# Recurrence gates in mixed PSUM banks: seven gate tiles per group of three channel chunks instead of ten

## The reference, cut to what matters

```
xb, gate = split(rmsnorm(x) @ w_in)                  # 1024 -> 2 x 1536
xb = causal_depthwise_conv(xb)                       # 4 taps
xs = xb.reshape(seq, 16 blocks, 96)
r = sigmoid(einsum('shi,hij->shj', xs, wr) + br)     # 16 blocks of 96 x 96
i = sigmoid(einsum('shi,hij->shj', xs, wi) + bi)
log_a = -8 * r * softplus(-lam);  a = exp(log_a)
b = sqrt(1 - a^2) * (i * xb)
hs[t] = a[t] * hs[t-1] + b[t]
x = x + (hs * silu(gate)) @ w_out
```

## Time and profile before

| what | us |
|---|---|
| median of 3 runs | 1112.67 |
| lowest and highest | 1112.06, 1564.1 |
| the profiled execution, its own time | 1113.04 |
| its span in the trace | 1111.2 |
| PE busy | 1098.6 (99%) |
| DVE busy | 769.9 (69%) |
| ACT busy | 558.6 (50%) |
| POOL busy | 249.9 (22%) |

### The profile page before, as it was taken

One profiled execution on the slowest core, in us unless ns is written; L12 is line 12 of the kernel. 1 busy time (PEld: TensorE's weight loads), 2 busy tenths in 40 slices (PEclk: granted clock), 3 DMA queues, 4 the chain that ended last, 5 costly groups with the idle time before them and its releaser, 6 DMA issues.

```text
span 1111.2 us, 14419 instructions
## 1 busy us (share of the span) xinstructions
PE 1098.6 (99%) x5216; PEld 867.9 (78%) x5216; DVE 769.9 (69%) x1220; ACT 558.6 (50%) x953; POOL 249.9 (22%) x226
## 2 busy tenths in 40 slices
PE   8999999999999999999999999999999999999997
PEld 6787787887677778867777878888878888888886
DVE  7887978787667765465445545547797687787796
ACT  6666567565676644254434433325453443453455
POOL 2022111330323412032112210003330440440443
PEclk9999999999999999999999999999999999999999
DMA  6322323323111123311222222223501701702401
GB/s 224 121 76 76 100 91 108 102 94 105 58 58 58 58 77 114 105 58 57 95 76 96 76 76 95 95 96 114 208 20 38 265 20 46 257 1 74 173 1 76
DMA packets 30054, 103.79 MB, mean 93 GB/s; under 512 B 3488, under 2 KB 3872, under 8 KB 29984
## 3 DMA queue, kind: packets, MB, share of 16 engines
q1 hardware_dynamic: 29552, 102.26, 26.8%
q10 hardware_dynamic: 432, 0.62, 0.2%
HBM read 100.24 MB, written 2.10 MB: 92 GB/s over the span
## 4 chain that ended last, share of the span: by engine, by line
PE 89%; DVE 6%; ACT 2%; issue 2%; DMA 1%; POOL 0%; SPq 0%; DVEq 0%; POOLq 0%; ACTq 0%
PE ps L903 22%; PE ps L904 22%; PE ps L905 22%; PE ps L863 4%; PE ps L864 4%; PE ps L865 4%; PE ps L1007 3%; PE ps L1022 3%; PE ps L1053 2%; DVE wl L1416 2%; PE ps L1047 1%; DMA raw<-wst 1%; DVE fl L1823 0%; PE ps L810 0%; DVE sg L1510 0%
## 5 line engine op out<-in xcount | busy, mean ns | idle before, releaser
L903 PE MATMUL ps<-xgh,wh 128*128 128x512 f32 x847 | 336.9, 398 | 1.8 <-ACT wh L1081 1.5
L905 PE MATMUL ps<-xgh,wl 128*128 128x512 f32 x847 | 330.3, 390 | 0.0
L904 PE MATMUL ps<-xgl,wh 128*128 128x512 f32 x847 | 330.0, 390 | 0.0
L1416 DVE TENSOR_TENSOR wl<-raw,wh 128x1024 fp32r<-128x1024 f32 x148 | 197.4, 1336 | 50.1 <-ACT wh L1092 49.5
L1092 ACT ACTIVATE wh<-raw 128x1024 fp32r<-128x1024 f32 x148 | 155.0, 1050 | 74.0 <-PE ps L905 53.8
L903 PEld LDWEIGHTS ps<-xgh,wh 128*128 128x128 f32 x847 | 159.1, 188 | 39.7 <-issue 6.5
L905 PEld LDWEIGHTS ps<-xgh,wl 128*128 128x128 f32 x847 | 159.0, 188 | 33.8
L904 PEld LDWEIGHTS ps<-xgl,wh 128*128 128x128 f32 x847 | 159.2, 188 | 32.4 <-issue 1.0
L1928 POOL TENSOR_SCALAR Pt<-Pt,stat 128x256 f32<-128x256 f32 (+2 forms) x128 | 75.0, 598 | 274.2 <-DVE stat L1672 199.0
L1300 ACT ACTIVATE Pt<-Pt,stat 128x256 f32<-128x256 f32 (+2 forms) x128 | 64.3, 503 | 60.9 <-DVE stat L1640 23.1
L863 PE MATMUL ps<-wh,fh 128*128 128x512 f32 x224 | 87.5, 391 | 1.9 <-DVE wl L1416 1.9
(11 more groups left out here) (244 smaller groups left out, 1798.6 us busy)
## 6 DMA issues: line engine op xcount, KB each, us to landing
raw<-wst SPq DMA_DIRECT2D x148, 512.0 KB, 3.5
b<-wdn SPq DMA_DIRECT2D x32, 512.0 KB, 6.8
bst<-nbias SPq DMA_DIRECT2D x8, 256.0 KB, 3.4
xt<-xT SPq DMA_DIRECT2D x3, 512.0 KB, 8.1
outT<-xtok SPq DMA_DIRECT2D x3, 512.0 KB, 2.6
sq<-fin SPq DMA_DIRECT2D x2, 256.0 KB, 4.3
cstt<-cst SPq DMA_DIRECT2D x1, 448.0 KB, 5.7
raw<-wst SPq DMA_DIRECT2D x1, 320.0 KB, 5.7
```

Source lines behind the costliest of these rows:

```text
L903: e.matmul(o, high, a, start=(k == 0), stop=False)
L904: e.matmul(o, high, b, start=False, stop=False)
L905: e.matmul(o, low, a, start=False, stop=stop).then_inc(tile_done, 1)
L1416: e.tensor_tensor(wl_t[:, v % NHL, :], src, f32(wh_t[:, v % NHL, :]), ALU.subtract).then_inc(lo_done, 1)
```

## The change: what it does, and the diff

A gate bank now holds halves of both gates. For each chunk one bank gets r of the chunk's lower 64 channels on partitions 0 to 63 and i of the same channels on partitions 64 to 127 (weights `r_i`), the other i of the upper 64 on partitions 0 to 63 and r of the upper 64 on 64 to 127 (`i_r`). The middle chunk needs then no full tile: its own 128 rows are two pieces of 64 rows with disjoint rows and different banks, one *pair* tile (pair 0), the pieces from its neighbours are pair 1, and what the neighbours need from it is pair 2. The low and the high chunk keep two full tiles each. In order: pair 0, full, full, pair 1, full, full, pair 2. The middle chunk is complete after the fourth tile, the low and the high one after the seventh.

ACT reads each chunk's two banks with four instructions on 64 partitions each (L1182 and L1185 before were one each on 128), two of which write to the other half of the partitions. The bias of i is stored rolled by 64 to lie beside its data.

The layer has 12 tiles fewer, one unit and a half. One unit keeps four tiles and is padded with zeros (`SHORT`), so that from the first tile of the next layer on the units hold the same tiles as before; in all there is one unit fewer. The ticks that depend on these places move: `gate_tick`, and the places of the unit splits in groups 1 to 3.

```
     def gates(self, g):
-        c = 3 * g
-        for own, over in (([("gr", c), ("gi", c)], 2), ([("gr", c + 1), ("gr", c + 2)], 0), ([], 3), ([("gi", c + 1), ("gi", c + 2)], 1)):
-            for name in own:
-                self.take(name)
-                self.tiles.append((name, 0, False))
...
+        middle, low, high = 3 * g, 3 * g + 1, 3 * g + 2
+        self.pair(g, 0, opens=(("gr", middle), ("gi", middle)))
+        self.full(low, "gr")
+        self.pair(g, 1, closes=(middle,))
+        self.full(high, "gi")
+        self.pair(g, 2, closes=(low, high))
+        for c in (middle, low, high):
+            self.n_act += 4
+            self.frees["gr", c] = ("act", self.n_act - 1)
+            self.frees["gi", c] = ("act", self.n_act)
...
         for g in range(4):
-            places = [end["silu", c] for c in range(3 * g, 3 * g + 3)] + [end["silu", 3 * g + 2] + 8]
+            ends = [end["silu", c] for c in range(3 * g, 3 * g + 3)] + [end["silu", 3 * g + 2] + 8]
+            taps = [ev_at["conv", c] + 2.0 for c in range(3 * g, 3 * g + 3)]
             if g == 0:
-                places = [end["conv", 2]] + places
+                places = [end["conv", 2]] + ends
+            elif g == 1:
+                places = [end["conv", 3]] + taps[1:] + ends
+            elif g == 2:
+                places = [end["conv", 6] - 3] + taps + ends
             else:
-                taps = [ev_at["conv", c] + 2.0 for c in range(3 * g, 3 * g + 3)]
-                places = [end["conv", 3 * g] - (3 if g > 1 else 0)] + taps + places[g < 2:]
+                places = taps + ends
...
-                UNIT_AT[u] = max(8.0 * u - 20.0, UNIT_AT[u - 1] + 5.0)
+                UNIT_AT[u] = max(ch.units[u][1] - 20.0, UNIT_AT[u - 1] + 5.0)
...
         def gate_tick(c):
-            return end["gi", c] + 1.2 + 3.5 * (c % 3 > 1)
+            return end["gi", c - c % 3] + 1.2 + (0.0, 3.0, 6.5)[c % 3]
...
-            def gates_over(g, n, high, low):
+            def gates_pair(g, n, high, low):
+                middle, below, above = 3 * g, 3 * g + 1, 3 * g + 2
+                if n == 0:
+                    bits = [(lo, middle, ("gr", middle)), (hi, middle, ("gi", middle))]
+                    for rows, k, name in bits:
+                        wait_bank(q, name)
+                elif n == 1:
+                    bits = [(slice(96, 128), below, ("gr", middle)), (slice(0, 32), above, ("gi", middle))]
+                    q.wait_ge(tile_done, ch.at_pair[g] + 1)
                 else:
+                    bits = [(lo, middle, ("gi", below)), (hi, middle, ("gr", above))]
...
             def gate(c):
-                e.activation(trr, bank[ch.bank["gr", c]], ACT.Tanh, scale=0.5, bias=drvc(HBR + c, HBR + c + 1)).then_inc(gate_read, 1)
-                q.wait_ge(tile_done, end["gi", c] + 1)
+                x_, y_ = bank[ch.bank["gr", c]], bank[ch.bank["gi", c]]
+                t_ = tii[c % 2]
+                r_, i_ = drvc(HBR + c, HBR + c + 1), drvc(HBI + c, HBI + c + 1)
+                e.activation(trr[lo, :], x_[lo, :], ACT.Tanh, scale=0.5, bias=r_[lo, :]).then_inc(gate_read, 1)
+                e.activation(trr[hi, :], y_[hi, :], ACT.Tanh, scale=0.5, bias=r_[hi, :]).then_inc(gate_read, 1)
                 q.wait_ge(ix_done, c - 1)
-                e.activation(tii[c % 2], bank[ch.bank["gi", c]], ACT.Tanh, scale=0.5,
-                             bias=drvc(HBI + c, HBI + c + 1)).then_inc(gate_read, 1)
+                e.activation(t_[lo, :], x_[hi, :], ACT.Tanh, scale=0.5, bias=i_[hi, :]).then_inc(gate_read, 1)
+                e.activation(t_[hi, :], y_[lo, :], ACT.Tanh, scale=0.5, bias=i_[lo, :]).then_inc(gate_read, 1)
```

More of the change, by code:

```diff
@@ L16 @@
 UT = 8
+SHORT = 4
 NRAW = 3
@@ L88, in __init__ @@
         self.end, self.ring, self.at, self.n_dve, self.n_act, self.user = {}, 7, 0, 0, 0, {}
-        self.at_over = {}
+        self.at_pair = {}
         self.units, self.unit_of = [], []
@@ L108, in run, with unit @@
             self.frees[name] = ("dve", self.n_dve)
[L110 to L114, removed]
+    def unit(self, kind, size, n=None):
+        stop = len(self.unit_of) + n if n else len(self.tiles)
+        while len(self.unit_of) < stop:
+            first = len(self.unit_of)
+            size = min(size, stop - first)
+            self.unit_of += [(len(self.units), s) for s in range(size)]
             self.units.append((kind, first, first + size - 1))
@@ L150, in gates, with full, pair @@
     def gates(self, g):
-        c = 3 * g
-        for own, over in (([("gr", c), ("gi", c)], 2), ([("gr", c + 1), ("gr", c + 2)], 0), ([], 3), ([("gi", c + 1), ("gi", c + 2)], 1)):
-            for name in own:
-                self.take(name)
-                self.tiles.append((name, 0, False))
[L158 to L166, removed]
+        middle, low, high = 3 * g, 3 * g + 1, 3 * g + 2
[8 more added lines that the diff above has]
+            self.frees["gi", c] = ("act", self.n_act)
+    def full(self, c, alone):
+        for kind in ("gr", "gi"):
+            self.take((kind, c))
+            self.tiles.append(((kind, c), 0, kind == alone))
+    def pair(self, g, n, opens=(), closes=()):
+        for name in opens:
+            self.take(name)
+        if n == 0:
+            self.at_pair[g] = len(self.tiles)
+        self.tiles.append((("pair", g, n), 0 if opens else 1, False))
+        for c in closes:
+            self.end["gr", c] = self.end["gi", c] = len(self.tiles) - 1
     def group(self, names, k, ks):
@@ L209, in gemm_plan @@
         ch.gates(g)
+    ch.unit(("ring",), UT)
     for j in range(6):
@@ L217, in gemm_plan @@
         ch.one(("wa", j), 12)
+    ch.unit(("ring",), SHORT, SHORT)
     ch.ring, ch.at = 3, 1
@@ L795, in conv_there @@
                 return xsh_t[:, c % 4, :], xsl_t[:, c % 4, :]
-            def gates_over(g, n, high, low):
[L799 to L802, removed]
-                else:
[L804 to L807, removed]
+            def gates_pair(g, n, high, low):
+                middle, below, above = 3 * g, 3 * g + 1, 3 * g + 2
+                if n == 0:
+                    bits = [(lo, middle, ("gr", middle)), (hi, middle, ("gi", middle))]
[4 more added lines that the diff above has]
+                    q.wait_ge(tile_done, ch.at_pair[g] + 1)
+                else:
+                    bits = [(lo, middle, ("gi", below)), (hi, middle, ("gr", above))]
                 bits = [(rows, *conv_there(k), bank[ch.bank[name]]) for rows, k, name in bits]
                 for rows, a, b, o in bits:
-                    e.matmul(o, high[rows], a[rows], start=False, stop=False)
+                    e.matmul(o, high[rows], a[rows], start=(n == 0), stop=False)
                 for rows, a, b, o in bits:
@@ L813, in gates_over @@
                 for rows, a, b, o in bits:
-                    done = e.matmul(o, low[rows], a[rows], start=False, stop=(n != 2))
+                    done = e.matmul(o, low[rows], a[rows], start=False, stop=(n != 0))
                 done.then_inc(tile_done, 1)
@@ L870, in gemm @@
                     u, s = ch.unit_of[t]
-                    if k == 0:
+                    if k == 0 and name[0] != "pair":
                         wait_bank(q, name)
@@ L889, in gemm @@
                     low = wl_t[:, u % NHL, blk(s)]
-                    if name[0] == "over":
-                        gates_over(name[1], name[2], high, low)
+                    if name[0] == "pair":
+                        gates_pair(name[1], name[2], high, low)
                         continue
@@ L1513, in gate @@
                 yield gate_tick(c) + 2.0
-                q.wait_ge(gate_read, 2 * c + 2)
+                q.wait_ge(gate_read, 4 * c + 4)
                 q.wait_ge(xsl_done, c + 1)
@@ L2037, in weight_stream, with r_i, i_r @@
         add(gate[3 * g:3 * g + 3])
[L2038 to L2051, removed]
+        def r_i(rows, first):
+            return np.concatenate([full[n, g, rows, first:first + 64] for n in (0, 1)], axis=1)
+        def i_r(rows, first):
+            return np.concatenate([full[n, g, rows, first:first + 64] for n in (1, 0)], axis=1)
+        pairs = np.zeros((3, 128, 128), np.float32)
+        pairs[0, 0:64], pairs[0, 64:128] = r_i(slice(128, 192), 128), i_r(slice(192, 256), 192)
+        pairs[1, 96:128], pairs[1, 0:32] = r_i(slice(96, 128), 128), i_r(slice(256, 288), 192)
+        pairs[2, 0:64], pairs[2, 64:128] = i_r(slice(128, 192), 64), r_i(slice(192, 256), 256)
+        add(pairs[0:1])
+        add(np.stack([r_i(slice(0, 128), 0), i_r(slice(0, 128), 64)]))
+        add(pairs[1:2])
+        add(np.stack([r_i(slice(256, 384), 256), i_r(slice(256, 384), 320)]))
+        add(pairs[2:3])
+    rest = wo[:2, 6:9].reshape(-1, 128, 128)
+    add(rest[:SHORT])
+    add(np.zeros((UT - SHORT, 128, 128), np.float32))
+    add(rest[SHORT:])
     add(wo[2:6, :9])
@@ L2111, in params @@
     put("br", cols(a["a_gate_r_b"][0])[:, CHUNKS])
-    put("bi", cols(a["a_gate_i_b"][0])[:, CHUNKS])
```

(1 more changed line is left out.)

4 lines of the change are left out of this document (2 added, 2 removed).

## The result

The changed kernel took 1130.27 us (median), the one before 1112.92 beside it: the ratio is 1.0157, with a 95% interval of 1.0145 to 1.017. It is slower by 17.3 us; forecast were 9.3 and at most 14. The profiled execution of the changed kernel took 1131.17 us, 0.9 more than the median; its span is 1129.2.

The account below looks back on a forecast made before the run. The loop of DVE, ACT and POOL was taken as the bound, PE just behind. Its terms, 2.8 - 1.6 + 3.4 + 3.4 - 1.3 + 3.4 + 0.8 - 1.6 = +9.3 us, gave 1122.0 us; range 1110 to 1127.

Parts of the forecast that it names:

- gates 0: Group 0's gates: half reads add 3.4 us on ACT, an earlier start saves 0.6, so the loop shifts +2.8 us.
- group 1, moved split: Group 1's first conv chunk: one unit split moves to the silu chunks, 2.7 won less 1.1, so -1.6 us.
- gates 1: Group 1's gates: the four half reads of each chunk cost ACT +3.4 us.
- gates 2, no unit behind them: Group 2's gates: +3.4 us for half reads, -1.3 because no unit is split directly behind them in group 3.
- gates 3 and the tail: Group 3's gates +3.4 us; then one unit's `wh` gone before the roots, its low part before a scan: +0.8.
- slack of PE at the end: At the layer's last `yl`, PE was not waiting before, so 1.6 us of the loop's lateness is absorbed: -1.6.
- The half reads: ACT's gate reads: four of 64 partitions at 0.57 us, 1.14 us more a chunk, 3.4 a group, 13.7 in all.
- The rival with PE as the bound: The loop has unseen slack and PE's 9.6 us of spared tiles are won: 1103 us, chance 0.07.
- The one with cheap half reads: ACT's half reads cost half each: -2.7 us, 1110; chance 0.21, shared with partly cheap reads or moved units worth more.
- ACT's gate phase: Expected profile sign: four tanh of 64 partitions per chunk, 0.57 us apart, the phase taking 12.6 us instead of 9.2.
- PE's clock: Rival: pauses halve the clock, up to 1148 us; 0 to 3 expected. Chance 0.06 with unseen stalls, 0.04 over 2%.
- The POOL window: Group 1's taps beside POOL's multiplying: if DVE and POOL lock out, the move wins 1.8, not 2.7; sum +10.2.

Follow-up runs that it names:

- the kernel with two full reads: The changed kernel with two reads of 128 partitions per chunk instead of four halves, leaving r and i mixed up (computes something else): 1110.54 us, ratio 0.9979.

## Why the prediction was wrong

The direction, the bound and the place were right; the range (1110 to 1127) missed 1130.27 because one term of the sum was too small and the bound above it was no bound. Term by term, the shift of the loop against the trace before:

| step | predicted | measured | where |
|---|---|---|---|
| gates 0 | +2.8 | +4.6 | first `ub` of group 1, 58.12 to 62.68 |
| group 1, moved split | -1.6 | -1.3 | its last `yl`, 90.72 to 93.95 (+3.2) |
| gates 1 | +3.4 | +5.0 | `yl`, +8.3 |
| gates 2, no unit behind them | +3.4 - 1.3 | +5.0 - 1.4 | `yl`, +11.9 |
| gates 3 and the tail | +3.4 + 0.8 | +5.1 + 0.3 | last `yl`, +17.3 |
| slack of PE at the end | -1.6 | -0.5 | `wa` tile, +16.8 |

**The half reads.** The prediction took "an instruction's time goes with its 512 elements per partition and not with the number of partitions" and called 2 x 0.57 = 1.14 us for a chunk the upper end. The first half held: a half read is under way as long as a full one. But 0.57 is the distance of two instructions that overlap, and this overlap was carried over to instructions of another shape without a row for it. It is lost at all four steps of the changed kernel, which take 0.69 to 0.71 us, 2.82 in all for 1.13: 1.7 us more a chunk. 12 x (1.70 - 1.14) = 6.7 of the 8.0 us by which 9.3 fell short. PE's row of 64 partitions was a witness for durations and was used for distances.

**The slack.** PE's next tile after the layer's last `yl` needs a weight unit too, and ACT splits that unit, the third of three in a row, right after the `yh` that `yl` waits for. It came late with the rest; the wait at 230.29 is for it. Before, the three splits ran from 209.93 to 212.87 us and the tile came at 213.52. So the 1.6 us were read off one of two suppliers, and the other had about half a us. That is 1.1 more. The remaining half us lies behind the layer, where nothing was changed: from the first `y2h` tile to the end of the span it is 870.5 us before and 871.6 after, and over the traces of all runs it lies between 870.5 and 872.0.

**What held.** The tiles (5.88 us for 5.87). No waits of DVE and ACT for PE. The moved splits: -1.3, -1.4 and +0.3 for -1.6, -1.3 and +0.8. The test that decided, that all waits between the three engines point away from PE, was the right one to make. The rival with PE as the bound was rightly given little. The one with cheap half reads gave 1110 and is what the kernel with two full reads shows (1110.54), but for full reads.

**The signs.** Of what the profile was to show, the gate phase of PE (5.9 us) came true, and so did that DVE and ACT never wait for PE. ACT's gate phase is 3 x 4.77 = 14.3 us, not 12.6, since its half reads start 0.70 us apart and not 0.57. Two `yl` of the same place lie 49.9 us apart, inside 48 to 50, but PE doesn't wait for them: in groups 2 and 3 it waits earlier, for DVE to evict `gu` (4.4 us before 142.62, 2.1 before 192.49), works through the gates at half clock and comes to the tile that needs `yl` when it is there. Only group 1's `yl` is waited for. PE's waits are 17.2 us in all and not 19.

**PE's clock.** It did fall. The stretch from 192 to 198 us, PE, PEld, DVE, ACT, POOL busy, clock, DMA:

```profile
192.00:198.00 6.00, 5.51 (x15) 3.53 (x16) 5.39 (x6) 4.20 (x7) 1.46 (x1) 0.51 0.35 128
```

and how PE came into another such stretch:

```profile
142.62 0.79 PE L924 MATMUL ps<-xsh,wh 128*128 128x512 f32 x1 [4.43 <-DVE gu L1505]
143.21 0.63 PE L925 MATMUL ps<-xsl,wh 128*128 128x512 f32 x1
143.64 0.63 PE L926 MATMUL ps<-xsh,wl 128*128 128x512 f32 x1
...
147.95 0.39 PE L926 MATMUL ps<-yh,wl 128*128 128x512 f32 x1
```

After a wait of 4.4 us the starts are 0.43 us apart instead of 0.23: 1.2 GHz and not 2.4, until a little before 147.95, where a matmul takes 0.39 again. The Trainium skill, TensorE: Matmul & The Clock Gate, section HAM oscillation — how this bites in real kernels, says that pauses re-throttle the array and that its work behind each of them starts at half speed. The trace agrees (0.51 in this stretch), but for one pause: behind the 3.1 us before 95.55 PE ran a us at 2.4 GHz first, and fell then. It cost next to nothing, since PE had time to spare ahead of the next late supplier: with 5.5 us more of PE's work in the pauses the mean clock of the span rose from 0.990 to 0.995 and the time stayed (1130.46 for 1130.27).

**The POOL window.** Group 1's first conv chunk after the change, DVE's three taps without the unit between them, the next chunk's two, and POOL's products:

```profile
64.41 2.32 DVE L1518 SCALAR_TENSOR_TENSOR xs<-ub,part,xs 128x512 f32<-128x512 f32 x3
...
68.47 3.37 DVE L1518 SCALAR_TENSOR_TENSOR xs<-ub,part,xs 128x512 f32<-128x512 f32 x2
...
66.31 4.98 POOL L1936 TENSOR_TENSOR xs<-xs,cc 128x512 f32<-128x512 f32 x3 [45.47 <-ACT cc L1227]
```

The first chunk's taps all started ahead of POOL's products and took 0.77 us each; two of the next chunk's took 3.37 beside them, where the earlier trace rows has 1.53 for two alone. The Trainium skill, SBUF — State Buffer, section Who interferes with whom, has it that the two engines lock each other out there. The trace agrees, and the prediction's middle way between winning all of the moved split and losing it to POOL (1.6 won) was near the 1.3 measured.

## What to carry to other kernels

Where two engines or groups of engines are nearly equal bounds, work taken from the one is worth little or nothing, however busy it is on the page; look at who waits for whom in the stage, and count what the edit puts on the other side for every repetition of the loop. Cost an instruction by the distance to the next start, and don't carry that distance over to another shape: if no row has two such instructions in sequence, take at least the full duration (0.68 us here; 0.69 to 0.71 were measured), not the overlapped 0.57. Slack at a place is the smallest over all its suppliers, and suppliers that are queued behind the same late instruction slip together.

## What the runs showed of the hardware

- ACT, tanh from PSUM of 512 elements: 0.66 to 0.69 us with 64 partitions, 0.66 to 0.74 with 128. Start to start 0.57 between two on the same 128 partitions, 0.59 between two on the same 64, 0.69 to 0.71 from one half to the other and from a half to all 128. From a square on all 128 to a read of the lower half it was 0.52 in the changed kernel, as from 128 to 128, and 0.64 in four others; why is open.
- With source and target in different halves all steps were 0.69 to 0.72, whichever of the two stayed the same.
- Where the program has an ACT instruction wait for the one just ahead of it to be done, the step was 0.89 us behind an 0.80 us `cc` (0.71 without the wait) and 0.71 behind a 0.67 us `trr` (0.57 without).
- PE's clock was at 1.2 GHz behind waits of 2.1, 2.6, 3.1 and 4.4 us in this kernel, and back at 2.4 between 2.8 and 6.4 us after work had begun again (from 73.12 to 75.9, from 142.62 to a little before 147.95, from 192.49 to 198.9); behind waits of 1.0, 1.2 and 1.7 us it stayed at 2.4.
